# Identity products on TensorE during five waits of a three-block kernel

## What is computed

```python
# block 1
h = layer_norm(x) * (1 + sc1) + sh1
x = layer_norm(ALPHA * x + g1 * token_mixer(h))       # long convolution and gated mixing
h = layer_norm(x) * (1 + sc2) + sh2
logits = h @ w_router + b_router                      # 32 experts, top 4, softmax of the four
x = layer_norm(ALPHA * x + g2 * experts(h, logits))
# block 2
xn = rms_norm(x)                                      # retention (8 heads) and a gated recurrence
x = rms_norm(x + concat(y_ret, y_lru) @ w_out)
# block 3
hg = rms_norm(x); x = x + gated_linear_attention(hg)
hs = rms_norm(x); x = x + grouped_state_space(hs)
out = rms_norm(x)
```

## Time and profile before

| | |
|---|---|
| median of 3 runs | 2367.45 us (2365.8 to 2368.61) |
| the profiled execution's own time | 2367.97 us |
| its span | 2366.2 us |
| mean granted clock of TensorE | 0.969 |
| TensorE busy | 2170.4 us, 92% of the span |
| VectorE, ScalarE busy | 749.6 us, 466.2 us |
| transfers | 591.29 MB, mean 250 GB/s |

### The profile page before, as it was taken

The page is one execution under the profiler, slowest core; times in us unless marked ns, Lnnn a source line. Parts: engine busy times, 40 slices in busy tenths (PEclk is TensorE's granted clock), DMA queues, the critical chain, the costliest instruction groups (busy, mean ns, idle before and its releaser), DMA issues.

```text
span 2366.2 us, 29984 instructions
## 1 busy us (share of the span) xinstructions
PE 2170.4 (92%) x11393; PEld 1144.2 (48%) x11394; DVE 749.6 (32%) x1831; ACT 466.2 (20%) x923; POOL 65.2 (3%) x79
## 2 busy tenths in 40 slices
PE   5999987999999998999988996997989997999998
PEld 4844444343333333333333334644464446888873
DVE  1596243222222221222222212342022255777100
ACT  1011111111111111111111101132021107886100
POOL 0000000000000000000000001000000000221000
PEclk8999997999999999999999998999989998999999
DMA  9544566769999999999966997442333241222240
GB/s 347 210 160 178 204 229 248 315 267 419 417 419 417 419 417 384 418 418 418 418 276 271 419 413 253 144 174 108 108 118 142 71 151 72 102 78 72 98 168 37
DMA packets 158855, 591.29 MB, mean 250 GB/s; under 512 B 5323, under 2 KB 6928, under 8 KB 125888
## 3 DMA queue, kind: packets, MB, share of 16 engines
q1 hardware_dynamic: 152512, 573.08, 61.7%
q0 software_dynamic: 4384, 16.40, 1.9%
q10 hardware_dynamic: 1887, 0.81, 0.1%
HBM read 589.23 MB, written 1.05 MB: 249 GB/s over the span
## 4 chain that ended last, share of the span: by engine, by line
PE 75%; DMA 14%; DVE 4%; ACT 3%; DVEq 2%; issue 2%; ACTq 0%; SPq 0%
PE PS L608 25%; PE PS L886 14%; DMA W<-in_w_gu 12%; PE PS L596 9%; PE PS L909 6%; PE PS L1084 4%; PE PS L833 2%; PE PS L922 2%; PE PS L1157 1%; PE PS L665 1%; DVE BIG L1877 1%; PE PS L850 1%; DVE BIG L1881 1%; DMA W<-in_w_mod 1%; PE PS L1145 1%
## 5 line engine op out<-in xcount | busy, mean ns | idle before, releaser
L608 PE MATMUL PS<-W,BIG 128*128 128x512 f32 x1344 | 583.3, 595 | 5.1 <-DVE BIG L2311 2.9
L886 PE MATMUL PS<-W,BIG 128*64 128x512 f32 x2048 | 451.8, 595 | 21.0 <-DMA W<-in_w_gu 20.8
L608 PEld LDWEIGHTS PS<-W,BIG 128*128 128x128 f32 x1344 | 255.8, 191 | 322.9 <-issue 316.4
L886 PEld LDWEIGHTS PS<-W,BIG 128*64 128x64 f32 x2048 | 142.1, 137 | 312.9 <-issue 270.8
L909 PE MATMUL PS<-W,BIG 128*64 128x512 f32 x1024 | 229.1, 600 | 6.9 <-ACT BIG L1363 6.9
L596 PE MATMUL PS<-BIG,W 128*128 128x256 f32 x1024 | 224.0, 381 | 1.4 <-ACT BIG L349 1.4
L596 PEld LDWEIGHTS PS<-BIG,W 128*128 128x128 f32 x1024 | 195.5, 191 | 29.6 <-ACT BIG L349 2.2
L1875 DVE TENSOR_SCALAR BIG<-PS 128x512 f32<-128x512 f32 (+1 forms) x38 | 24.7, 649 | 381.7 <-PE PS L886 355.9
L909 PEld LDWEIGHTS PS<-W,BIG 128*64 128x64 f32 x1024 | 71.1, 138 | 144.1 <-issue 126.4
L1084 PE MATMUL PS<-BIG,W 128*128 128x256 f32 x512 | 118.8, 386 | 0.3 <-ACT BIG L1517 0.3
L1358 ACT ACTIVATE BIG<-BIG 128x512 f32<-128x512 f32 x32 | 20.2, 630 | 488.8 <-DVE BIG L1875 488.8
(11 more groups left out here) (451 smaller groups left out, 1922.0 us busy)
## 6 DMA issues: line engine op xcount, KB each, us to landing
W<-in_w_gu SPq DMA_DIRECT2D x128, 2048.0 KB, 17.6
W<-in_w_dn SPq DMA_DIRECT2D x64, 2048.0 KB, 19.2
W<-in_w_in SPq DMA_DIRECT2D x24, 2048.0 KB, 13.8
W<-in_w_mod SPq DMA_DIRECT2D x12, 2048.0 KB, 9.5
W<-in_gla_w_in SPq DMA_DIRECT2D x10, 2048.0 KB, 7.6
W<-in_s_w_in SPq DMA_DIRECT2D x8, 2048.0 KB, 8.8
W<-in_s_w_glu SPq DMA_DIRECT2D x8, 2048.0 KB, 8.1
W<-in_w_out SPq DMA_DIRECT2D x6, 2048.0 KB, 7.9
```

The costliest lines, as they stand in the source:

```text
L608: ins = pe.matmul(ps[:, t, :], lhs(i * KT + k)[:, t * P:(t + 1) * P], w[:, k, :], start=i + k == 0, stop=last_chunk and k == KT - 1)
L886: ins = pe.matmul(PS[hh[h], g, :], XET[:, k, :], gu_w(k)[:, g * D + h * CH:g * D + (h + 1) * CH], start=False, stop=k == KT - 1, skip_grou ...
```

## The change

A helper `keep_active` issues a number of products of the identity with the first 256 columns of `K` (the identity and a triangular matrix) into an accumulator bank whose content has been read; nothing reads what they write. It is called at five places of TensorE's program: in the routing, in three parts with a wait for `neg_max` and one for `exp_ready` between them; after the experts, in three parts with a wait for the sixth `std_ready` and one for the first `row_ready` between them; and ahead of the waits for "yr", "hg" and "hs". Other engines' programs are the same.

```diff
--- before.py
+++ after.py
@@ -674,6 +674,11 @@
                         ins = pe.transpose(PS[:, 4 + n % 2, j * P:(j + 1) * P], src[t][:, (4 * h + j) * P:(4 * h + j + 1) * P], ident)
                     ins.then_inc(tp_ready, 1)
 
+            def keep_active(bank, count):
+
+                for _ in range(count):
+                    pe.matmul(PS[:, bank, 0:T], ident, K[:, C_ID:C_ID + T], start=True, stop=True, skip_group_check=True)
+
             def columns_ready(name):
                 pe.wait_ge(tp_copied, TB[name] + dict(TRANSPOSES)[name])
 
@@ -758,6 +763,11 @@
                                     start=k == 0, stop=k == KT - 1)
             ins.then_inc(ev("logits_done"), 1)
 
+            keep_active(4, 8)
+            pe.wait_ge(ev("neg_max"), 1)
+            keep_active(4, 5)
+            pe.wait_ge(ev("exp_ready"), 1)
+            keep_active(4, 12)
             pe.wait_ge(ev("sel_ready"), 1)
             pos = PS[:, 7, 0:3 * NE].rearrange("p (a e) -> p a e", a=3)
             pe.matmul(pos[:, 0, :], K[:, C_TRI:C_TRI + P], SEL[:, 0, :], start=True, stop=True)
@@ -941,6 +951,11 @@
                 expert(e, False)
             expert(NE - 1, True)
 
+            keep_active(0, 32)
+            pe.wait_ge(std_ready, 6)
+            keep_active(0, 14)
+            pe.wait_ge(ev("row_ready"), 1)
+            keep_active(0, 24)
             for t in range(TT):
                 pe.wait_ge(ev("rows_ready"), NORMED["xn"] + t + 1)
                 row_to_columns("xn", t, row(2)[:, t])
@@ -987,6 +1002,7 @@
                 pe.matmul(o[:, P:T], s_[:, P:T], V2[:, 0, c], start=True, stop=False)
                 pe.matmul(o[:, P:T], s_[:, T:T + P], V2[:, 1, c], start=False, stop=True).then_inc(ev("o_done"), 1)
             pe.wait_ge(ev("o_copied"), 8)
+            keep_active(6, 38)
             pe.wait_ge(ev("yr_ready"), 1)
             rows_to_columns("yr", [O2[:, 0], O2[:, 1]])
             columns_ready("yr")
@@ -994,6 +1010,7 @@
             for i in range(2):
                 dense(f"w2o{i}", lambda k: YRT[:, k, :] if k < KT else R2[:, k - KT, :])
 
+            keep_active(6, 36)
             for t in range(TT):
                 pe.wait_ge(ev("rows_ready"), NORMED["hg"] + t + 1)
                 row_to_columns("hg", t, row(9)[:, t])
@@ -1064,6 +1081,7 @@
             for i in range(2):
                 dense(f"go{i}", lambda k: OGT[:, k, :])
 
+            keep_active(6, 24)
             for t in range(TT):
                 pe.wait_ge(ev("rows_ready"), NORMED["hs"] + t + 1)
                 row_to_columns("hs", t, row(9)[:, t])
```

## The result

The changed kernel took 2387.49 us (median of 4 runs, 2383.06 to 2392.76), the kernel before 2367.26 us (4 runs). The ratio is 1.0086 with a 95% interval of 1.0064 to 1.0108: slower, by 20.2 us. The four runs of the changed kernel lie 9.7 us apart, and the interval leaves room for 15 to 26 us. The forecast was 2388 us. The profiled execution of the changed kernel is the shortest of the four, 2383.06 us with a span of 2381.2.

A forecast was written before the change was run, and what follows sets the result against it. The prediction took TensorE, busy for 92% of the span, as the bound. Overruns of 33.7 us less 12.9 us given back by the warm clock made +20.8 us, so 2388 us, range 2381 to 2396.

The forecast's parts named there:

- The price of a product: All five places on TensorE: each added f32 product is two instructions, 0.434 us at full clock, 0.868 at half.
- Overruns: All five waits: every group of products outlasts its wait and delays the work behind; together 33.7 us lost.
- What is given back: Work behind the five waits: starting at full instead of half clock saves 12.9 us together.
- Is an overrun hidden anywhere?: Behind the experts none hidden; the routing's net 2.0 us counted, zero at the least if the expert loop's transfers swallow it.
- no transfer is waited for there: Behind the experts: no wait for transfers, and DVE and ACT get their next work from TensorE, so overruns are not hidden.
- (a): Rival, all groups: a product costs one instruction's 0.217 us, so 11.7 us faster, 2356; chance 0.05.
- (b): Rival, all groups: the products don't raise or hold the clock, nothing is given back, +116 us, 2483; chance 0.04.
- (c): Rival, routing: only this group stays at half clock, 14.6 us in place of 2.0, 2401; chance 0.04.

The follow-up runs named there:

- the kernel with the sixth wait: Changed kernel with all counts halved and six products added in a wait ahead of the spreading of "g2"; 2350.3 us, ratio 0.9936 to the kernel before.
- with transposes: Changed kernel with transposes of the identity in place of the products, twice the counts, 386 in all; 2354.12 us, ratio 0.9949 to the kernel before.
- the longest routing group: Changed kernel with only the routing group kept, at 8, 5 and 20 products; 2377.48 us, ratio 1.0045 to the kernel before.

## Why the prediction was right

The mechanism was right: every group overran its wait, and the overrun less what the warm clock gave back is the loss. The total, 2388 against 2387.49 us, is closer than such a sum, or four runs 9.7 us apart, can promise; that closeness is luck, as the last steps show. The steps:

**The price of a product** (0.434 us, two instructions): right. 140 instructions in 30.48 us are 0.218 us each, 0.435 a product; the doubled counts gave 0.432 in this stage.

**Overruns.** Predicted ends against measured: the routing block 12.5 us long, measured 12.6 (364.83 to 377.43), with the rise after 3.5 us where I had taken 3.3. The others 30.4, 16.5, 15.6 and 10.4 us; measured 30.3, 16.5, 15.5 and 10.4 from the start of each block to the next instruction.

**What is given back.** Stage by stage, net: routing +2.0 predicted, +2.08 measured; "xn" +9.5, +9.4; "yr" +5.8, +6.3 (the products start 0.5 us late, after the last copy of the retention's output: the bracket of 0.47 at 1652.63); "hg" +2.5, +2.4. Line 1003 (now 1020) took 3.63 us, predicted 3.5. For "hs" neither the whole stretch nor its own part repeats. The rows of before and after in the first profiles, from the last dense product on:

```profile
1895.70 56.90 PE L608 MATMUL PS<-W,BIG 128*128 128x512 f32 x128 [0.74 <-ACT BIG L1466]
...
1973.46 0.60 PE L1098 MATMUL PS<-K,MISC 128*128 128x128 f32 x4
```

```profile
1911.85 55.20 PE L608 MATMUL PS<-W,BIG 128*128 128x512 f32 x128 [0.74 <-ACT BIG L1484]
...
1981.88 7.07 PE L1102 MATMUL PS<-BIG,W 128*128 128x256 f32 x32
1988.79 0.60 PE L1116 MATMUL PS<-K,MISC 128*128 128x128 f32 x4
```

From the end of line 608 to the next `turn_b`: 1973.46-1952.60 = 20.9 us before, 1988.79-1967.05 = 21.7 us after, +0.9 against +1.0 predicted. But the second profiles have 19.1 and 23.4 us, +4.3. The 21.7 us are a part at full clock throughout; in the second profile of the changed kernel the clock fell behind the transposes, at a wait of 1.7 us that had left it up in the first, and line 1102 took 8.49 us in place of 7.07. So the +0.9 is one pair out of two, and its match is chance; the mean of both is +2.6.

The same rows show how line 608, untouched by the change, moves: it took 1.7 us less in this profile than before, since there the clock fell for some 3.4 us behind the short waits ahead of it. In the second profile of the changed kernel it took 56.62 us. These two places are 3.1 of the 4.5 us between its two profiles.

**Is an overrun hidden anywhere?** For the routing this step has the size wrong, as far as the profiles tell. I counted its net 2.0 us in full, with zero as the bound. The stage did grow by 2.08 us, but the loop shrank by 2.0 to 2.2 in both profiles, and in the kernel with the routing group alone the time is that of before, with an interval that doesn't exclude the 2.0. The reason that I gave for the bound, that transfers might set the loop's end, is refuted. Stage and loop together are 1067.6 us before, but 1078 in two kernels with more products, and 1061.95 in the kernel with the sixth wait: no end is fixed at 1067.6. The rows show another reason: at the first expert with additional blocks line 833 (843) runs partly at half clock before, and not after.

```profile
469.00 8.80 PE L833 MATMUL PS<-W,BIG 128*32 128x256 f32 x128 [0.60 <-DVE BIG L1885]
```

```profile
469.60 7.11 PE L843 MATMUL PS<-W,BIG 128*32 128x256 f32 x128 [0.60 <-DVE BIG L1903]
```

That is 1.7 of the 2.0 us. The sum of the stages in the mean of the two profiles of each kernel is then +2.1-2.1+9.4+6.3+2.4+2.5-0.5 = +20.1 us, the 2.5 being the stretch to "hs" with its chance and the -0.5 what lies ahead of the routing and behind `turn_b`. The forecast's +20.8 was thus met with the routing's 2.0 us missing, 1.5 us more at "hs" and 0.5 more at "yr": errors that cancelled. What decides where the clock falls in the loop stays open. The places where the profiles differ are few: the first additional block (1.7 us, in both profiles of before and in three kernels with no or a halved routing group), behind the first gather (4.5 us, with halved counts, with transposes and with the longest routing group), and the last expert (2.8 us more, once). The loop took 1045.3 to 1053.2 us over all kernels, it repeated within 0.2 us for the same kernel, and it follows neither from whether there is a routing group (1045.7, 1048.05 and 1053.2 with one alone) nor from that group's length in an order that I can name.

One premise of this step was wrong: "no transfer is waited for there", behind the experts. TensorE waits for none, but VectorE does: its row above stands 2.9 us behind the end of ScalarE's root (1444.12 to 1444.32), held up by the gain vector. This cost the forecast nothing, because the group ran far past it. But in before the wait of 19.49 us is set by this transfer at its end, and not by VectorE and ScalarE alone; a kernel that fetched the vector earlier could shorten it by up to 2.9 us, an estimate from these two rows that no run tests.

**Rivals.** (a), that a product costs 0.217 us, is refuted; but its time, 2356, is what the halved counts gave (2356.88), since its groups would have been as long. (b) and (c) are refuted by the windows above.

## What to carry to other kernels

Filling a wait on an engine that works in order is only free up to the wait's end; behind it every product is paid in full. So before adding any, take from the trace what one source line costs (an f32 product here is two instructions), multiply by the count, and lay it beside the bracket of the wait; a raised mean clock and a raised busy share prove nothing. What warm-up products can give is bounded by half of the time that the work behind the wait runs at half clock: here 1 to 4 us a place (and none in one of them when the wait itself grew by 1.5 us), worth having at four fifths of the wait's length and a loss of 20 us in five places at one and a half times of it or more.

## What the runs showed of the hardware

The clock also fell while TensorE was busy all the time. With halved counts it was at full clock through the first gather and fell at 383.3, behind 12 instructions with 32 stationary rows (line 787), with no idle time:

```profile
378.00:383.00 5.00, 5.00 (x22) 2.76 (x22) 2.38 (x18) 1.88 (x2) 0.00 (x0) 1.00 0.01 3
383.00:384.00 1.00, 1.00 (x5) 0.70 (x6) 0.40 (x1) 0.00 (x0) 0.00 (x0) 0.68 0.00 0
384.00:391.00 7.00, 7.00 (x20) 2.29 (x20) 2.35 (x12) 0.00 (x0) 0.00 (x0) 0.50 0.00 0
```

It cost 4.5 us at that place: from the first gather to the first scatter 44.4 us against 39.5 to 40.5 in the kernels where it did not fall. With the 2.0 us that the first additional block did not cost, the loop was 2.5 us longer than before, and that ate most of the 2.8 us that the routing had gained. The same happened with the transposes and with the longest routing group. So a busy TensorE isn't enough, and single executions of a kernel with short stalls differ by several microseconds (2362.4 to 2371.3 in 17 runs of before) for this reason at least in part: between two profiles of before, one stretch of unchanged code differed by 3.5 us.
